# Output projection, two normalisations, turn and router products in one stage over tiles of 128 tokens

## The chip, the cores and the metric

The kernel runs on one core of a Trainium2 chip. The metric is the time of one execution in microseconds (us); the median of three runs of the kernel before is 3086.5 us (3078.68 to 3088.62).

## The reference, cut to what matters

Two transformer blocks follow one another on 512 tokens of width 1024, batch 1, all in float32. Each block is a mixer and then a mixture of experts. The change concerns the end of each mixer and the first step of each mixture of experts.

```python
# block one, after the mixer's two branches (attention and LRU)
mixed = jnp.concatenate([rms_norm(attn, g_attn), rms_norm(lru, g_lru)], axis=-1)
mix = jnp.einsum('bse,ed->bsd', mixed, w_out)                    # 512x1024 @ 1024x1024
x = layer_norm(DEEPNORM_ALPHA * x + (1.0 + gt_m) * mix, ln1_g[l], ln1_b[l])
u = layer_norm(x) * (1.0 + sc_f) + sh_f
#   router of block one: u @ w_grp (4 columns), u @ w_exp (16 columns), then softmax and top k

# block two, after its two attention branches
y = (sigmoid(g_a) * (o_a @ w_out_a) + sigmoid(g_b) * (o_b @ w_out_b)) @ w_o   # the last one: 512x1024 @ 1024x1024
x = x + gt1 * rmsnorm(y, g_post_mix[i])
h2 = rmsnorm(x, g_pre_ffn[i]) * (1 + sc2) + sh2
#   router of block two: h2 @ w_router (32 columns), then top 4 and softmax
```

## The kernel before

The part of the program that the change touches is, in block one, this chain of stages; in block two it is the same with other names:

1. `norm_branches` ("nb1", line 1111) normalises the two branches and turns them into the stationary operand `mixed`; SP loads the first two chunks of `w_out` meanwhile. In block two its place is taken by `turn` ("tz", line 496).
2. `out_projection` ("out1", line 1384), in block two `project` ("out2"): the weight goes by in four chunks of 256 output columns. For each chunk the four token tiles are multiplied (16 outputs of 128 x 256, 24 matmuls each), so that a tile of tokens is complete only when the last chunk has gone by. In block one VectorE takes each output from PSUM with lines 1391 and 1392, in block two ScalarE copies it (line 2807).
3. `normalise` ("n1b" / "n2y", line 413): statistics of all four tiles, then the scaling of all four, on VectorE.
4. `normalise` ("m1n" / "m2n"), called from `moe_inputs`: the same again with the modulation's rows; each tile is stored to `xn_dram`.
5. `turn` ("m1t" / "m2t"): 32 transposes of 128 x 128 on TensorE, copied out of PSUM by ScalarE (line 531).
6. `route` ("r1" / "r2", line 1414): SP loads the router's weights, TensorE makes 32 products of 128 x 20 (block two 128 x 32) at line 1468, VectorE adds the bias at line 1511 and a long chain of small operations follows, which ends in the list of experts for the next stage.

## Time and profile before

| | |
|---|---|
| median of three runs | 3086.5 us (3078.68 to 3088.62) |
| the profiled execution's own time | 3086.95 us |
| its span in the profile | 3085.2 us |
| PE, PEld, DVE, ACT, POOL busy | 82%, 67%, 73%, 51%, 11% of the span |
| mean granted TensorE clock | 0.908 |
| HBM traffic | 692.73 MB read, 39.39 MB written |

Engines: PE is TensorE's matmuls, PEld its weight loads, DVE is VectorE, ACT is ScalarE, POOL is GpSimd, SP issues most DMAs. The clock is a share of 2.4 GHz and has two levels, 1.00 and 0.50 (1.2 GHz). The page's 40 slices are 77 us each; the two stretches in question lie in slices 6 and 7 and in slices 21 and 22, where DMA is at 1 or 2 tenths; the slices with DMA at 9 tenths are the two expert loops. The chain that ended last on the page covers only the program's last few operations, so the stretches are read from the timeline and the windows.

### The profile page before, as it was taken

The page shows a single profiled execution, that of the slowest core. Times are in us where ns is not written, and L with a number is a line of the kernel's source. Part 1 is how long each engine was busy: PE and PEld are TensorE (multiplying, and loading weights), DVE is VectorE, ACT ScalarE, POOL GpSimd, SP SyncE. Part 2 cuts the span into 40 slices and gives each one's busy share as a digit, 9 for nine tenths or more (in the row PEclk, how much of TensorE's full clock was granted, in tenths as well). Part 3 has the DMA queues.
Part 4 walks back from the last instruction along what each step waited for, and adds up shares of the span by engine and source line. Part 5 has one row for each costly group of instructions (what it writes and reads, how often), then busy time and mean ns, then how long its engine had stood idle before and what let it go on. Part 6 is the DMA issues. An engine that isn't in the chain of part 4 may idle for free. (4 is left out here: it accounts for less than half of the span.)

```text
span 3085.2 us, 37604 instructions
## 1 busy us (share of the span) xinstructions
PE 2534.3 (82%) x12807; PEld 2078.8 (67%) x12807; DVE 2238.1 (73%) x2195; ACT 1573.6 (51%) x1462; POOL 339.5 (11%) x277
## 2 busy tenths in 40 slices
PE   2968773599991999778873599999999999999991
PEld 2852663477771999567673477777777777777771
DVE  5637754588885440678535699999999999999985
ACT  2213620477763531546230366776777777776770
POOL 1110200033330000000000001111011111112110
PEclk9989885799995999889985699999999999999995
DMA  5846111699993341000221699999999999999984
GB/s 194 271 137 222 23 61 56 244 362 377 370 361 131 94 134 49 1 28 1 82 69 43 217 352 367 369 368 365 363 368 366 364 366 360 366 365 366 367 332 156
DMA packets 254856, 731.70 MB, mean 237 GB/s; under 512 B 29772, under 2 KB 69931, under 8 KB 252527
## 3 DMA queue, kind: packets, MB, share of 16 engines
q1 hardware_dynamic: 228180, 645.62, 57.9%
q0 software_dynamic: 21984, 80.77, 6.9%
q10 hardware_dynamic: 4608, 4.20, 0.4%
q8 instruction: 51, 0.84, 0.1%
q14 instruction: 33, 0.27, 0.0%
HBM read 692.73 MB, written 39.39 MB: 237 GB/s over the span
## 5 line engine op out<-in xcount | busy, mean ns | idle before, releaser
L48 PE MATMUL psum_all<-sb_ring_r,sb_arena_r 128*128 128x512 f32 (+1 forms) x2912 | 1070.9, 368 | 0.0
L154 DVE TENSOR_TENSOR sb_ring_r<-sb_ring,sb_hi_ring 128x2048 fp32r<-128x2048 f32 x297 | 674.7, 2288 | 207.4 <-ACT sb_hi_ring L145 201.8
L47 PE MATMUL psum_all<-sb_hi_ring,sb_arena_r 128*128 128x512 f32 (+1 forms) x1880 | 666.9, 355 | 53.7 <-DVE sb_ring_r L154 46.6
L49 PE MATMUL psum_all<-sb_hi_ring,sb_arena_r 128*128 128x512 f32 (+1 forms) x1880 | 661.0, 352 | 0.0
L48 PEld LDWEIGHTS psum_all<-sb_ring_r,sb_arena_r 128*128 128x128 f32 x2912 | 558.5, 192 | 91.0
L145 ACT ACTIVATE sb_hi_ring<-sb_ring 128x2048 fp32r<-128x2048 f32 x297 | 564.4, 1914 | 108.0 <-DMA sb_ring<-in_w_gu_dram 34.1
L154 DVE TENSOR_TENSOR sb_ring_r<-sb_ring,sb_arena_r 128x2048 fp32r<-128x2048 f32 x258 | 582.0, 2285 | 31.5 <-ACT sb_arena_r L145 30.9
L145 ACT ACTIVATE sb_arena_r<-sb_ring 128x2048 fp32r<-128x2048 f32 x258 | 485.4, 1911 | 199.9 <-DMA sb_ring<-in_w_gu_dram 192.5
L47 PEld LDWEIGHTS psum_all<-sb_hi_ring,sb_arena_r 128*128 128x128 f32 x1880 | 362.3, 193 | 110.3 <-DVE sb_ring_r L154 51.9
L47 PE MATMUL psum_all<-sb_arena_r 128*128 128x512 f32 x1032 | 417.3, 404 | 11.8 <-DVE sb_ring_r L154 6.8
L49 PE MATMUL psum_all<-sb_arena_r 128*128 128x512 f32 x1032 | 408.2, 396 | 0.0
L49 PEld LDWEIGHTS psum_all<-sb_hi_ring,sb_arena_r 128*128 128x128 f32 x1880 | 361.2, 192 | 51.1
L47 PEld LDWEIGHTS psum_all<-sb_arena_r 128*128 128x128 f32 x1032 | 194.9, 189 | 68.7 <-DVE sb_ring_r L154 27.5
L49 PEld LDWEIGHTS psum_all<-sb_arena_r 128*128 128x128 f32 x1032 | 195.8, 190 | 45.7
L1723 POOL DMA_INDIRECT y_dram<-sb_arena x52 | 89.3, 1718 | 989.9 <-ACT sb_arena L1874 989.9
L1709 POOL COPY sb_arena<-sb_ids 128x1 int32 (+1 forms) x54 | 28.7, 531 | 1034.2 <-POOLq L70 467.5
L47 PE MATMUL psum_all<-sb_arena_r,sb_hi_ring 128*128 128x512 f32 (+2 forms) x232 | 90.1, 389 | 38.5 <-DVE sb_hi_ring L781 30.6
L1849 ACT ACTIVATE sb_arena_r<-psum_all 128x1024 fp32r<-128x1024 f32 x54 | 55.2, 1022 | 114.6 <-PE psum_all L1752 96.2
L1924 DVE TENSOR_TENSOR sb_arena_r<-psum_all,sb_arena_r 128x1024 fp32r<-128x1024 f32 x54 | 65.6, 1214 | 62.8 <-ACT sb_arena_r L1849 62.8
L512 PE MATMUL psum_all<-sb_ident,sb_arena 128*128 128x128 f32 x128 | 29.1, 394 | 91.1 <-PEq L70 89.3
L1869 ACT ACTIVATE sb_arena_r<-psum_all 128x1024 fp32r<-128x1024 f32 (+1 forms) x52 | 45.8, 881 | 106.7 <-PE psum_all L1761 106.5
L1714 POOL DMA_INDIRECT sb_arena<-xn_dram,sb_arena x54 | 92.9, 1720 | 65.4 <-POOL sb_arena L1709 40.8
(393 smaller groups left out, 3159.1 us busy)
## 6 DMA issues: line engine op xcount, KB each, us to landing
sb_ring<-in_w_gu_dram SPq DMA_DIRECT2D x272, 1024.0 KB, 6.9
sb_ring<-in_w_dn_dram SPq DMA_DIRECT2D x136, 1024.0 KB, 9.5
sb_ring<-in_w_e_gate_dram SPq DMA_DIRECT2D x36, 1024.0 KB, 7.3
sb_ring<-in_w_e_up_dram SPq DMA_DIRECT2D x36, 1024.0 KB
sb_ring<-in_w_e_down_dram SPq DMA_DIRECT2D x36, 1024.0 KB, 7.4
sb_ring<-in_w_in_dram SPq DMA_DIRECT2D x27, 1024.0 KB, 7.0
sb_arena<-in_w_ada_dram POOLq DMA_DIRECT2D x16, 1024.0 KB, 5.8
sb_ring<-in_w_mod_dram SPq DMA_DIRECT2D x16, 1024.0 KB, 5.2
```

The source lines that it names most:

```text
L47: eng.matmul(out, a[0], b[0], start=start, stop=False)
L48: eng.matmul(out, a[0], b[1], start=False, stop=False)
L49: return eng.matmul(out, a[1], b[0], start=False, stop=stop)
L145: act.activation(s.hi[c % len(s.hi)], s.raw[c % len(s.raw)], ACT.Copy).then_inc(s.hi_made, 1)
L154: dve.tensor_tensor(s.lo[c % len(s.lo)], s.raw[c % len(s.raw)], s.hi[c % len(s.hi)].bitcast(F32), ALU.subtract).then_inc(s.lo_made, 1)
L512: ins = pe.transpose(k.psum[:, i % 2, t * P:(t + 1) * P], src[:, t, i * P:(i + 1) * P], k.ident[:])
L1709: pool.tensor_copy(idx, R.ids[:, bass.ds(j, 1)]).then_inc(s.idx, 1)
L1714: pool.indirect_dma_start(xg, None, m.x, bass.IndirectOffsetOnAxis(ap=idx.bitcast(U32), axis=0)).then_inc(s.gathered, 16)
L1723: pool.indirect_dma_start(m.y, bass.IndirectOffsetOnAxis(ap=to_row.bitcast(U32), axis=0), ysb.rearrange("p h n -> p (h n)"), None).then_in ...
L1849: act.activation(part, banks, ACT.Copy).then_inc(s.x_hi, 1)
L1869: act.activation(part, banks, ACT.Copy).then_inc(s.h_hi, 1)
L1924: dve.tensor_tensor(part, banks, turned_banks(x_hi[p], KD)[0].bitcast(F32), ALU.subtract).then_inc(s.x_lo, 1)
```

## The change

The stages 2 to 5 of the list above and the router's products of stage 6 become one stage, `project_and_normalise`, called once per block. The weight is loaded in four chunks of 256 rows (all 1024 columns) instead of four chunks of 256 columns, all four of them in the stage before (`ahead`), and its high and low halves all stay in SBUF. TensorE then multiplies one tile of 128 tokens with the whole weight (48 matmuls of 128 x 512 into two PSUM banks), and VectorE and ScalarE normalise that tile twice while TensorE works on the next. Each finished tile is transposed by TensorE (8 transposes), copied by ScalarE and multiplied with the router's weights (8 products). The rows of gain and shift and the router's weights are loaded at the start of this stage. In block two the sums of squares come from ScalarE (`Square` with an accumulator) and no longer from VectorE's batch statistics. `route` begins with the addition of the bias.

The diff, cut to its core ("first" is true in block one):

```diff
-                  ahead=[column_chunk(a["w_out"][0], 256 * h) for h in range(AHEAD)],
+                  ahead=[row_chunk(a["w_out"][0], c) for c in range(4)],
-    out_projection(nc, k, "out1", a["w_out"][0], mixed, k.gate_rows[0:1, :], k.arena[:, 0:D])
-    normalise(nc, k, "n1b", k.x, TT, D, k.x, True, 1e-5, gain=a["ln1_g"][0], bias=a["ln1_b"][0])
-def out_projection(nc, k, name, w, mixed, gate_dram, gate):
...
+    rows = [k.rows[:, 0, :]] + [k.arena[:, 20480 + D * i:20480 + D * (i + 1)] for i in range(4)]
+    project_and_normalise(nc, k, "out1", True, mixed, k.arena_r[:, 8192:10240], area(10240, 2, D),
+                          list(zip(rows, (k.gate_rows[0], a["ln1_g"][0], a["ln1_b"][0], k.gate_rows[5], k.gate_rows[4]))),
+                          [(a["w_grp"][0], a["b_grp"][0]), (a["w_exp"][0], a["b_exp"][0])], area(0, TT, D), area(4096, KD, T))
...
+def row_chunk(w, c):
+    return w[256 * c:256 * c + 256, :].rearrange("(k p) n -> p k n", p=P)
...
+def project_and_normalise(nc, k, name, first, mixed, fourth, tmp, rows, routers, xn, u):
...
+    hi = [k.hi_ring[:, i, :] for i in range(HI_SLOTS)] + [fourth]
+    raw, lo = [k.ring[:, i, :] for i in range(4)], [k.ring_lo[:, i, :] for i in range(4)]
+    two = lambda t: x_rows(k.psum[:, 2 * (t % 2):2 * (t % 2) + 2, :])
+    x_rows = lambda ap: ap.rearrange("p a n -> p (a n)")
...
+        @block.sync
+        def _(sp):
+            for dst, src in rows:
+                sp.dma_start(dst, src.partition_broadcast(P)).then_inc(s.rows, 16)
+            c = 0
+            for ws, bs in routers:
+                n = ws.shape[1]
+                sp.dma_start(router[:, :, c:c + n], ws.rearrange("(k p) n -> p k n", p=P),
+                             allow_slow_non_contiguous=True).then_inc(s.router, 16)
+                sp.dma_start(bias[:, c:c + n], bs.partition_broadcast(P)).then_inc(s.router, 16)
+                c += n
+            for t in range(TT):
+                sp.wait_ge(s.done, t + 1)
+                sp.dma_start(k.xn_dram[t * P:(t + 1) * P, :], xn[:, t, :]).then_inc(s.stored, 16)
+            sp.wait_ge(s.stored, 16 * TT)
+            sp.wait_ge(s.router, 32 * len(routers))
+        @block.tensor
+        def _(pe):
+            def multiply(t):
+                if t >= 2:
+                    pe.wait_ge(s.emptied, t - 1)
+                for kk in range(KD):
+                    c, j = kk // 2, kk % 2
+                    if t == 0 and j == 0:
+                        pe.wait_ge(s.w_lo, c + 1)
+                    a = [x[:, kk, t * P:(t + 1) * P] for x in mixed]
+                    for half in range(2):
+                        b = [x[c][:, j * D + 512 * half:j * D + 512 * half + 512] for x in (hi, lo)]
+                        ins = split3(pe, k.psum[:, 2 * (t % 2) + half, :], a, b, kk == 0, kk == KD - 1)
+                ins.then_inc(s.multiplied, 1)
+            def turn_tile(t):
+                pe.wait_ge(s.done, t + 1)
+                if t >= 1:
+                    pe.wait_ge(s.put, t)
+                for kk in range(KD):
+                    ins = pe.transpose(k.psum[:, 4 + kk // 4, (kk % 4) * P:(kk % 4) * P + P], xn[:, t, kk * P:(kk + 1) * P],
+                                       k.ident[:])
+                ins.then_inc(s.turned, 1)
+            def score(t):
+                if t == 0:
+                    pe.wait_ge(s.router, 32 * len(routers))
+                pe.wait_ge(s.put, t + 1)
+                for kk in range(KD):
+                    ins = pe.matmul(k.psum[:, 7, t * W:(t + 1) * W], u[:, kk, t * P:(t + 1) * P], router[:, kk, :],
+                                    start=kk == 0, stop=kk == KD - 1)
+            multiply(0)
+            multiply(1)
+            multiply(2)
+            turn_tile(0)
+            multiply(3)
+            score(0)
+            for t in range(1, TT):
+                turn_tile(t)
+                score(t)
+        @block.scalar
+        def _(act):
+            def square(t, src, out, total, done):
+                act.activation(out, src, ACT.Square, accum_out=total[:, t:t + 1]).then_inc(done, 1)
+            def root(t, inv, out, ready, done):
+                act.wait_ge(ready, t + 1)
+                act.activation(out[:, t:t + 1], inv[:, t:t + 1], ACT.Sqrt).then_inc(done, 1)
+            def put(t):
+                act.wait_ge(s.turned, t + 1)
+                act.activation(u[:, :, t * P:(t + 1) * P], x_rows(k.psum[:, 4:6, :]).rearrange("p (k n) -> p k n", k=KD),
+                               ACT.Copy).then_inc(s.put, 1)
+            def mixed_in(t):
+                if not first:
+                    act.wait_ge(s.multiplied, t + 1)
+                    square(t, two(t), tmp[:, t % 2, :], squares1, s.squared1)
+                root(t, inv1, root1, s.inverted1, s.rooted1)
+            def taken_out(t):
+                if not first:
+                    act.wait_ge(s.mixed, t + 1)
+                    square(t, k.x[:, t, :], xn[:, t, :], squares2, s.squared2)
+                root(t, inv2, root2, s.inverted2, s.rooted2)
+            for c in range(4):
+                act.activation(hi[c], raw[c], ACT.Copy).then_inc(s.w_hi, 1)
+            mixed_in(0)
+            taken_out(0)
+            mixed_in(1)
+            taken_out(1)
+            mixed_in(2)
+            put(0)
+            taken_out(2)
+            mixed_in(3)
+            put(1)
+            taken_out(3)
+            put(2)
+            put(3)
+        @block.vector
+        def _(dve):
+            link = chain(dve, s.chain)
+            def invert(t, src, scale, eps, inv, ready):
+                link(dve.tensor_scalar(inv[:, t:t + 1], src, scale, eps, ALU.mult, ALU.add))
+                dve.reciprocal(inv[:, t:t + 1], inv[:, t:t + 1]).then_inc(ready, 1)
+            def centred(t, inv, ready):
+                x = k.x[:, t, :]
+                dve.bn_stats(stats[:, t, 0, :], x[:, 0:512])
+                link(dve.bn_stats(stats[:, t, 1, :], x[:, 512:D]))
+                link(dve.bn_aggr(aggr[:, t, :], stats[:, t, :, :]))
+                invert(t, aggr[:, t, 1:2], 1.0, 1e-5, inv, ready)
+            def mix_in(t):
+                x, part = k.x[:, t, :], tmp[:, t % 2, :]
+                if first:
+                    gate = rows[0][0]
+                    dve.wait_ge(s.multiplied, t + 1)
+                    dve.tensor_tensor(part, two(t), gate, ALU.mult).then_inc(s.emptied, 1)
+                    dve.wait_ge(s.emptied, t + 1)
+                    link(dve.scalar_tensor_tensor(out=x, in0=x, scalar=ALPHA, in1=part, op0=ALU.mult, op1=ALU.add))
+                    centred(t, inv1, s.inverted1)
+                    return
+                dve.wait_ge(s.squared1, t + 1)
+                invert(t, squares1[:, t:t + 1], 1.0 / D, 1e-6, inv1, s.inverted1)
+            def normalise(t):
+                x, part = k.x[:, t, :], tmp[:, t % 2, :]
+                if first:
+                    gain, shift = rows[1][0], rows[2][0]
+                    link(dve.scalar_tensor_tensor(out=x, in0=x, scalar=aggr[:, t, 0:1], in1=gain, op0=ALU.subtract,
+                                                  op1=ALU.mult))
+                    dve.wait_ge(s.rooted1, t + 1)
+                    link(dve.scalar_tensor_tensor(out=x, in0=x, scalar=root1[:, t:t + 1], in1=shift, op0=ALU.mult,
+                                                  op1=ALU.add))
+                    centred(t, inv2, s.inverted2)
+                    return
+                gain = rows[0][0]
+                dve.wait_ge(s.rooted1, t + 1)
+                dve.scalar_tensor_tensor(out=part, in0=two(t), scalar=root1[:, t:t + 1], in1=gain, op0=ALU.mult,
+                                         op1=ALU.mult).then_inc(s.emptied, 1)
+                dve.wait_ge(s.emptied, t + 1)
+                dve.tensor_tensor(x, x, part, ALU.add).then_inc(s.mixed, 1)
+            def mean_out(t):
+                if not first:
+                    dve.wait_ge(s.squared2, t + 1)
+                    invert(t, squares2[:, t:t + 1], 1.0 / D, 1e-6, inv2, s.inverted2)
+            def take_out(t):
+                x, out, scale, shift = k.x[:, t, :], xn[:, t, :], rows[3 - (not first)][0], rows[4 - (not first)][0]
+                dve.wait_ge(s.rooted2, t + 1)
+                if first:
+                    link(dve.scalar_tensor_tensor(out=out, in0=x, scalar=aggr[:, t, 0:1], in1=scale, op0=ALU.subtract,
+                                                  op1=ALU.mult))
+                    dve.scalar_tensor_tensor(out=out, in0=out, scalar=root2[:, t:t + 1], in1=shift, op0=ALU.mult,
+                                             op1=ALU.add).then_inc(s.done, 1)
+                    return
+                link(dve.scalar_tensor_tensor(out=out, in0=x, scalar=root2[:, t:t + 1], in1=scale, op0=ALU.mult,
+                                              op1=ALU.mult))
+                dve.tensor_tensor(out, out, shift, ALU.add).then_inc(s.done, 1)
+            for c in range(4):
+                dve.wait_ge(s.w_hi, c + 1)
+                dve.tensor_tensor(lo[c], raw[c], hi[c].bitcast(F32), ALU.subtract).then_inc(s.w_lo, 1)
+            dve.wait_ge(s.rows, 16 * len(rows))
+            if not first:
+                link(dve.tensor_tensor(rows[0][0], rows[0][0], rows[1][0], ALU.mult))
+            for t in range(TT):
+                mix_in(t)
+                if t >= 1:
+                    take_out(t - 1)
+                normalise(t)
+                mean_out(t)
+            take_out(TT - 1)
...
         def _(pe):
-            pe.wait_ge(s.loaded, 32 * len(routers))
-            for t in range(TT):
-                for kk in range(KD):
-                    ins = pe.matmul(k.psum[:, 0, t * W:(t + 1) * W], u[:, kk, t * P:(t + 1) * P], w[:, kk, :],
-                                    start=kk == 0, stop=kk == KD - 1)
-            ins.then_inc(s.scored, 1)
...
-            dve.wait_ge(s.scored, 1)
-            psum = k.psum[:, 0, 0:TT * W].rearrange("p (t w) -> p t w", t=TT)
+            psum = k.psum[:, 7, 0:TT * W].rearrange("p (t w) -> p t w", t=TT)
...
-def moe_inputs(nc, k, name, centre, eps, scale, shift):
...
-    normalise(nc, k, name + "n", k.x, TT, D, xn, centre, eps, gain=scale, bias=shift,
-              store=[k.xn_dram[t * P:(t + 1) * P, :] for t in range(TT)])
-    turn(nc, k, name + "t", xn, TT, KD, None, None, None, None, plain=u)
-    return u
...
 def block_one_moe(nc, k, a):
-    u = moe_inputs(nc, k, "m1", True, 1e-5, k.gate_rows[5], k.gate_rows[4])
     k.route.max_items = 23
-    route(nc, k, "r1", u, [(a["w_grp"][0], a["b_grp"][0]), (a["w_exp"][0], a["b_exp"][0])], 16, 2, 4)
+    route(nc, k, "r1", 16, 2, 4)
...
-    y = area(12288, TT, D)
-    turn(nc, k, "tz", z, TT, KD, None, None, *zt, order=from_grid,
-         ahead=[column_chunk(a["w_o_2"][0], 256 * h) for h in range(AHEAD)])
-    project(nc, k, "out2", [dict(src=column_chunk(a["w_o_2"][0], 256 * h), uses=[use_t(y, 0, 256 * h, zt, T)])
-                            for h in range(D // 256)], ahead=AHEAD)
-    normalise(nc, k, "n2y", y, TT, D, k.x, False, 1e-6, gain=a["g_post_mix_2"][0], gate=k.gate_rows[2])
+    turn(nc, k, "tz", z, TT, KD, None, None, *zt, order=from_grid, ahead=[row_chunk(a["w_o_2"][0], c) for c in range(4)])
+    rows = [k.arena[:, 20480 + D * i:20480 + D * (i + 1)] for i in range(4)]
+    project_and_normalise(nc, k, "out2", False, zt, k.arena_r[:, 16384:18432], area(18432, 2, D),
+                          list(zip(rows, (a["g_post_mix_2"][0], k.gate_rows[2], k.gate_rows[7], k.gate_rows[6]))),
+                          [(a["w_router_2"][0], a["b_router_2"][0])], area(0, TT, D), area(12288, KD, T))
```

How TensorE's list stands at the end of the stretch in block one, before: the projection, then in the stages after it ("L67" and the line behind it are the barrier) the 32 transposes of stage 5 and the 32 router products of stage 6.

```order
L48 MATMUL psum_all<-sb_ring_r,sb_arena_r 128x256
L49 MATMUL psum_all<-sb_hi_ring,sb_arena_r 128x256
L67 UNCONDITIONAL_BRANCH
L506 UNCONDITIONAL_BRANCH
L512 MATMUL psum_all<-sb_ident,sb_arena 128x128 x32
L67 UNCONDITIONAL_BRANCH
L1463 UNCONDITIONAL_BRANCH
L1468 MATMUL psum_all<-sb_arena 128x20 x32
```

The same place after the change, from the last matmul of the fourth token tile on (L1467 is the transpose of a tile, L1476 its router products):

```order
L49 MATMUL psum_all<-sb_arena_r 128x512
L1476 MATMUL psum_all<-sb_rows,sb_arena 128x20 x8
L1467 MATMUL psum_all<-sb_ident,sb_arena 128x128 x8
L1476 MATMUL psum_all<-sb_rows,sb_arena 128x20 x8
L1467 MATMUL psum_all<-sb_ident,sb_arena 128x128 x8
L1476 MATMUL psum_all<-sb_rows,sb_arena 128x20 x8
L1467 MATMUL psum_all<-sb_ident,sb_arena 128x128 x8
L1476 MATMUL psum_all<-sb_rows,sb_arena 128x20 x8
L67 UNCONDITIONAL_BRANCH
```

Three of the four transposes and all router products stand behind the last projection matmul; only the first tile's transpose has moved up, in front of the fourth tile's matmuls.

VectorE's list in block one, before, from the end of the projection to the route: each kind of operation for all tiles, in a stage of its own.

```order
L1392 SCALAR_TENSOR_TENSOR sb_x<-sb_x,sb_pair 128x256
L67 UNCONDITIONAL_BRANCH
L442 UNCONDITIONAL_BRANCH
L447 BN_STATS sb_small<-sb_x 128x6 x8
L450 BN_AGGR sb_small<-sb_small 128x2 x4
L453 TENSOR_SCALAR sb_small<-sb_small 128x4
L458 RECIPROCAL sb_small<-sb_small 128x4
L466 SCALAR_TENSOR_TENSOR sb_x<-sb_x,sb_small,sb_rows 128x1024 x4
L472 SCALAR_TENSOR_TENSOR sb_x<-sb_x,sb_small,sb_rows 128x1024 x4
```

After, the operations for the second tile (L1550 and L1552 take it from PSUM, L1585 and L1587 finish the tile before it, L1562 and L1565 scale it):

```order
L1550 TENSOR_TENSOR sb_arena<-psum_all,sb_rows 128x1024
L1552 SCALAR_TENSOR_TENSOR sb_x<-sb_x,sb_arena 128x1024
L1540 BN_STATS sb_small<-sb_x 128x6
L1541 BN_STATS sb_small<-sb_x 128x6
L1542 BN_AGGR sb_small<-sb_small 128x2
L1535 TENSOR_SCALAR sb_small<-sb_small 128x1
L1536 RECIPROCAL sb_small<-sb_small 128x1
L1585 SCALAR_TENSOR_TENSOR sb_arena<-sb_x,sb_small,sb_arena 128x1024
L1587 SCALAR_TENSOR_TENSOR sb_arena<-sb_arena,sb_small 128x1024
L1562 SCALAR_TENSOR_TENSOR sb_x<-sb_x,sb_small,sb_arena 128x1024
L1565 SCALAR_TENSOR_TENSOR sb_x<-sb_x,sb_small,sb_arena 128x1024
```

The work of four stages now stands tile by tile in one list, and a tile's last two operations come behind the first ones of the next tile.

## Rows read from the trace of the kernel before

**Rows 1.** Timeline: start, us, engine, line, operation; where the two stretches begin and end.
```profile
412.21 3.71 ACT L145 ACTIVATE sb_hi_ring<-sb_ring 128x2048 fp32r<-128x2048 f32 x2 [2.97 <-PEq L70]
526.53 0.24 DVE L1511 TENSOR_TENSOR sb_arena<-psum_all,sb_arena 128x80 f32<-128x80 f32 x1 [30.11 <-PE psum_all L1468]
...
1560.02 3.71 ACT L145 ACTIVATE sb_hi_ring<-sb_ring 128x2048 fp32r<-128x2048 f32 x2 [1.44 <-PEq L70]
1676.28 0.29 DVE L1511 TENSOR_TENSOR sb_arena<-psum_all,sb_arena 128x128 f32<-128x128 f32 x1 [29.30 <-PE psum_all L1468]
```

**Rows 2.** Windows, block one: length, PE, PEld, DVE, ACT, POOL busy; clock, DMA.
```profile
411.90:464.30 52.40, 46.45 (x384) 46.25 (x384) 22.38 (x36) 7.55 (x4) 0.00 (x0) 0.93 0.17 51
464.30:480.60 16.30, 0.00 (x0) 0.00 (x0) 15.24 (x22) 0.21 (x1) 0.00 (x0) 0.59 0.18 64
480.60:500.60 20.00, 0.04 (x1) 0.07 (x2) 15.24 (x22) 0.21 (x1) 0.00 (x0) 0.50 0.43 158
500.60:508.00 7.40, 6.21 (x32) 4.91 (x32) 0.00 (x0) 4.60 (x8) 0.00 (x0) 0.71 0.01 2
508.00:526.50 18.50, 13.84 (x64) 13.73 (x64) 0.00 (x0) 1.28 (x1) 0.00 (x0) 0.60 0.07 5
```

**Rows 3.** Timeline of PE: start of both projections, and 512-column matmuls in the expert loop.
```profile
416.50 0.58 PE L47 MATMUL psum_all<-sb_hi_ring,sb_arena_r 128*128 128x256 f32 x1 [22.06 <-DVE sb_ring_r L154]
419.63 0.28 PE L49 MATMUL psum_all<-sb_hi_ring,sb_arena_r 128*128 128x256 f32 x1
...
1564.31 0.58 PE L47 MATMUL psum_all<-sb_hi_ring,sb_arena_r 128*128 128x256 f32 x1 [7.52 <-DVE sb_ring_r L154]
1569.96 0.28 PE L49 MATMUL psum_all<-sb_hi_ring,sb_arena_r 128*128 128x256 f32 x1
...
579.88 0.39 PE L48 MATMUL psum_all<-sb_ring_r,sb_arena_r 128*128 128x512 f32 x1
580.11 0.39 PE L49 MATMUL psum_all<-sb_hi_ring,sb_arena_r 128*128 128x512 f32 x1
```

**Rows 4.** Timeline of DVE in the stage that combines block one's experts, tile by tile.
```profile
960.14 1.23 DVE L2160 TENSOR_TENSOR sb_arena<-sb_arena,sb_rows 128x1024 f32<-128x1024 f32 x1
...
962.66 0.69 DVE L2162 BATCH_NORM_STATS2 sb_small<-sb_x 128x6 f32<-128x512 f32 x1
...
964.50 1.28 DVE L2156 SCALAR_TENSOR_TENSOR sb_arena<-sb_arena,sb_weight 128x1024 f32<-128x1024 f32 x1
...
970.18 1.26 DVE L2172 SCALAR_TENSOR_TENSOR sb_x<-sb_x,sb_small,sb_rows 128x1024 f32<-128x1024 f32 x1
...
972.68 1.28 DVE L2156 SCALAR_TENSOR_TENSOR sb_arena<-sb_arena,sb_weight 128x1024 f32<-128x1024 f32 x1
```

**Rows 5.** Timeline of ACT in the same stage: a square with its accumulator.
```profile
989.40 1.06 ACT L2126 ACTIVATE sb_arena<-sb_x 128x1024 f32<-128x1024 f32 x1 [2.30 <-DVE sb_x L2174]
990.36 0.19 ACT L2126 ACTIVATION_READ_ACCUMULATOR sb_arena<-sb_x 128x1 f32 x1
```

**Rows 6.** The page's groups that read two PSUM banks in the expert loops.
```profile
L1849 ACT ACTIVATE sb_arena_r<-psum_all 128x1024 fp32r<-128x1024 f32 x54 | 55.2, 1022 | 114.6 <-PE psum_all L1752 96.2
L1924 DVE TENSOR_TENSOR sb_arena_r<-psum_all,sb_arena_r 128x1024 fp32r<-128x1024 f32 x54 | 65.6, 1214 | 62.8 <-ACT sb_arena_r L1849 62.8
```

**Rows 7.** Timeline of PE: the last 8 transposes of block one's turn.
```profile
505.83 1.16 PE L512 MATMUL psum_all<-sb_ident,sb_arena 128*128 128x128 f32 x8 [0.18 <-ACT sb_arena L531]
```

**Rows 8.** Timeline of DVE: the first operation after a barrier.
```profile
464.66 4.84 DVE L447 BATCH_NORM_STATS2 sb_small<-sb_x 128x6 f32<-128x512 f32 x8 [0.79 <-PEq L70]
```

**Rows 9.** Windows (last two columns: DMA share, GB/s): row broadcasts; chunks of w_o.
```profile
482.00:486.00 4.00, 0.00 (x0) 0.00 (x0) 3.97 (x8) 0.00 (x0) 0.00 (x0) 0.50 0.80 256
...
1552.00:1554.00 2.00, 1.87 (x8) 1.35 (x8) 1.03 (x2) 1.94 (x5) 0.00 (x0) 0.50 1.03 327
```

**Rows 10.** Timeline of SP: the loads ahead, in block one and in block two.
```profile
383.88 1.04 SPq L1124 DMA_DIRECT2D sb_ring<-in_w_out_dram  x2
...
1548.49 1.75 SPq L123 DMA_DIRECT2D sb_ring<-in_w_o_dram  x2
```

47 lines of the change are left out of this document (19 added, 28 removed).

## The prediction

> **What bounds the kernel now.** I read the page first. The chain of waits there covers only the program's tail, so it says nothing about the middle. I went to the timeline of each engine around the two projections, then to the windows. A stage starts only after a barrier, so inside each stretch every microsecond between its first and last instruction is on the path. Each stretch begins where ScalarE rounds the first chunk of the projection's weight and ends where VectorE adds the router's bias, behind which the unchanged route runs: 526.53 - 412.21 = 114.3 us in block one and 1676.28 - 1560.02 = 116.3 us in block two [rows 1]. The windows of block one [rows 2] show the engines taking turns: 52.4 us in which TensorE is busy for 46.45 and VectorE for 22.38; two stretches of 16.3 and 20.0 us with VectorE alone (15.24 in each; the second also waits for stores); 7.4 us of transposes; 18.5 us of router products, 13.84 of them busy and the rest a wait for the router's weights. In a stretch of 114.3 us TensorE has 66.5 us of work and VectorE 52.9 (the columns added up), so about half can go if the two overlap. Everything outside the stretches keeps its instructions.
>
> **What the profile bases the sum on.** The profiled execution took 3086.95 us by itself, its span and the little that lies around it, and the median of the runs is 3086.5: I subtract from 3086.95 and expect no offset between that and a median.
>
> **The parts, block one.** All times below are on the clock of the trace before.
>
> Start. The first chunk has 128x2048 values as before, so TensorE's first matmul stays at 416.50 [rows 3]. Two further chunks are now loaded by the stage before. That stage begins its loads at 383.88 [rows 10] and ends at the barrier before 412.21; 4.2 MB at the 327 GB/s of rows 9 are 12.8 us plus about 1.5 until data flow, so they are in by 399: no cost. If that cover were gone, they would cost up to 12 us.
>
> Matmuls. 384 of 256 columns become 192 of 512. The start-to-start time of 512 columns at the full clock is 580.11 - 579.88 = 0.233 us [rows 3], together 44.8 us. Before, TensorE began cold and ran at the high level from 419.63, 3.1 us later [rows 3]; half of that is lost, 1.6 us. VectorE delivers a low half in about 2.4 us (twice the 1.21 of rows 6, the width being double) against 2.8 us or more of matmuls per chunk, so tile 0 doesn't wait. Tile 0 is complete at 429.2; tile 3 at 416.5 + 44.8 + 1.6 + 1.2 (the first tile's 8 transposes in between [rows 7]) = 464.1. So the product costs what it cost.
>
> VectorE per tile. Taking the tile from PSUM, adding, statistics and inverse: from 960.14 to 964.50 the same seven operations take 4.36 [rows 4], with the multiply reading PSUM, which costs 1.21 while TensorE streams [rows 6]. Scaling: two operations, 972.68 - 970.18 = 2.5 [rows 4], then statistics 964.50 - 962.66 = 1.84 [rows 4]: 4.35 with the link. Finishing: 2.5. Together 11.2 us, the same as TensorE's 48 x 0.233 = 11.2 per tile: the two are even, and VectorE has slack only through the transposes. At the end it owes for tile 3: 4.36, then tile 2's finish 2.5, 4.35, 2.5, so it is done at 464.3 + 13.7 = 478.0.
>
> Tail of TensorE. Its list is in order: router products of tile 0, then transpose, copy, products for tiles 1, 2, 3. A tile's products are 16 of the 64 instructions in 13.84 us [rows 2], 3.5 us, at the low level. A transpose of a tile is 1.16 at the high level [rows 7]; the other 24 of the 32 took 5.05, and I take 2.0 at the low level, an estimate from these. The copy is 1.02 [rows 6] plus 0.2 of handover. ScalarE's copy of tile 1 stands behind its root for tile 3, which waits for VectorE's first 4.36 us: 469.0. From there: copy 470.1, products 473.5, transpose 475.4, copy 476.9, products 480.4, transpose 482.4 (VectorE's tile 3 was ready at 478.0, so it is not waited for), copy 483.5, products 487.1. A barrier and the first instruction behind it cost 0.8 to 0.9 [rows 8]: the bias is added at 488.0 instead of 526.5. Gain 38.5 us.
>
> Loads in the stage. Five rows of 512 KB at 256 GB/s [rows 9] are 10.2 us, so 424.2 with the start, before tile 0 is complete at 429.2; the router's weights follow and are wanted after 464: no cost. Each is now issued ahead of its need, where it was waited for in stage 6 (18.50 - 13.84 = 4.7 us of rows 2, part of the gain). The four stores ride beside the next tile; the last one is issued at 478.0 and is over before 487. If the rows landed at 158 GB/s, the mean of the window with stores [rows 2], they would be in at 431, a 2 us delay of VectorE that the tail of TensorE hides.
>
> **The parts, block two.** Here the stage before is short and the loads are not hidden. The issue begins at 1548.49 [rows 10]; 4.2 MB at 327 GB/s end at about 1562.3, and that stage used to end some 0.8 before 1560.02, at 1559.2. The stretch starts 3.0 us later, at 1563.0 (bounds 0 and 13 more, the latter at half that rate). Then: first matmul 4.3 later [rows 3], 44.8 + 1.2, and 5.65 us of cold start [rows 3], half lost, 2.8: tile 3 complete at 1616.1. VectorE has four wide operations per tile instead of six plus statistics, ScalarE two squares of 1.06 + 0.19 [rows 5]; a tile takes them about 8 us against TensorE's 11.2, so both wait for TensorE. After tile 3: square 1.4, inverse 0.4, tile 2's finish 2.5, scaling 2.5, square 1.5, inverse and root 0.8, finish 2.5: done at 1627.9. TensorE's own list takes longer: products of tile 0 to 1617.9, transpose 1619.1, copy 1620.2, products 1623.8, transpose and copy 1627.0, products 1630.5, transpose and copy 1633.7, products 1637.2, barrier: 1638.1 instead of 1676.3. Gain 38.2 us.
>
> Sum: 3086.95 - 38.5 - 38.2 = 3010.
>
> **A rule on the clock, weighed.** The window 500.60:508.00 holds transposes as TensorE's only work, and its mean clock is 0.71; it starts at 0.50, so the clock rose while transposing. The next window is router products alone, busy for 13.84 us, and has a mean of 0.60, so the clock fell before them and stayed at 1.2 GHz although the engine was never idle [rows 2]. The Trainium skill ("TensorE: Matmul & The Clock Gate", Part 4: PE-mode transpose) says that the full clock doesn't engage for transposes. This trace, whose transposes are of float32, doesn't agree. By the rule the tail is at 1.2 GHz throughout, which is my sum; the rows leave it open.
>
> **Rivals.**
> (1) The tail runs at 2.4 GHz. For: the tail starts warm, and transposes alternate with products [rows 2]. Against: products alone ran at the low level. Price: three products at 1.75 less and three transposes at 0.85 less, then the end is set by VectorE: in block one 478.0 + 1.2 + 1.1 + 1.75 + 0.4 + 0.9 = 483.4, in block two 1627.9 + 5.3 = 1633.2. Time 3001.
> (2) Transfers hold the stages back: four chunks through the short stage of block two at half the rate (9 us more), and in block one rows that land late, 2 to 4 us. For: DMA was idle there before, so no row shows 6 MB in a queue. Against: 327 GB/s with two chunks in flight. Time about 3023.
> (3) TensorE stays at 1.2 GHz during the matmuls as well. For: it now waits for VectorE more often, since a tile costs both 11.2 us. Price: 512 columns at 1.2 GHz are 0.427 us, so 192 of them 82 us, 35 more than in my sum: block one ends at 524 and block two at 1674, 2 us gained in each: 3083, no change. Against: in the projection before, the clock was at 0.93 with the same waits of VectorE on the other side. It decides only if VectorE were late by some microseconds in every tile. The Trainium skill ("TensorE: Matmul & The Clock Gate", HAM oscillation) warns of just this: gaps between groups of matmuls send the clock down again and again. No gap longer than the transposes is in my schedule, so by this rule too the matmuls stay warm.
> (4) Slower than before: VectorE's and ScalarE's wide operations slow down by a factor f while TensorE fills the other two PSUM banks. Block one then ends at 439 + 45 f, block two at about 1591 + 34 f. At f = 2.5 that is 551 and 1676: 25 us lost in block one, nothing gained in block two, time 3111. It turns to a loss from f = 2.2. Against: VectorE's 1.21 and ScalarE's 1.02 from two PSUM banks were measured beside a busy TensorE [rows 6], f = 1.
>
> **How the numbers follow.** Forecast 3010, chance 0.63, own range 3003 to 3017 (cold start 3 to 6 us, load 0 to 4 more, handovers). Rival 1: 0.16; rival 2: 0.17; rival 3: 0.02; rival 4: 0.02. The range 2998 to 3029 takes in the first three. Faster by over 0.3% (9 us, about what this kernel's measurement tells from no change): 0.96. Same: 0.02. Slower: 0.02.
>
> **What would show it.** In the changed kernel's timeline: the first 512-column matmul 4.3 us after the stage's first rounding; tiles 11.2 us apart; VectorE idle for under 2 us per tile in block one and for 3 or more in block two; the clock of the window behind the last matmul (0.5: forecast; 1.0: rival 1); bias additions 76 and 75 us after the stages' start; the stage before block two's longer by 3 us. It would be wrong if the fourth tile's matmuls waited for VectorE, or if an expert loop changed its length.

## The result

| | before | changed kernel |
|---|---|---|
| median | 3087.49 us (3078.68 to 3088.62, 4 runs) | 3000.43 us (2997.26 to 3005.29, 4 runs) |
| ratio, 95% interval | | 0.9723, 0.971 to 0.9737 |
| profiled execution, its span | 3086.95, 3085.2 us | 2997.26, 2995.5 us |
| mean granted clock | 0.908 | 0.921 |
| PE, PEld, DVE, ACT, POOL busy | 82%, 67%, 73%, 51%, 11% | 84%, 68%, 74%, 53%, 11% |
| HBM read, written | 692.73, 39.39 MB | 692.73, 39.39 MB |

The forecast was 3010 us, between 2998 and 3029. The median lies 9.6 us under the point, inside that range, and 2.6 us under the narrower range of 3003 to 3017 that I gave for the stage's own terms. The mechanism was the one forecast. The median alone couldn't have said so: it is the time that rival 1 gave (3001), and the traces show that rival 1's tail didn't come. The two medians differ by 87 us, more than the change is worth: what follows puts it at 80 to 82 us.

The two stretches of the program, from ScalarE's first rounding of the projection's weight to VectorE's addition of the router's bias, in the timeline of the changed kernel (start, us, engine, line, operation; in brackets the idle time before it and what ended it). They answer to [rows 1]:

```profile
409.35 5.51 ACT L1516 ACTIVATE sb_hi_ring<-sb_ring 128x2048 fp32r<-128x2048 f32 x3 [2.98 <-PEq L70]
484.60 0.24 DVE L1688 TENSOR_TENSOR sb_arena<-psum_all,sb_rows 128x80 f32<-128x80 f32 x1 [9.41 <-PEq L70]
1512.77 3.71 ACT L1516 ACTIVATE sb_hi_ring<-sb_ring 128x2048 fp32r<-128x2048 f32 x2 [3.56 <-PEq L70]
1585.61 0.29 DVE L1688 TENSOR_TENSOR sb_arena<-psum_all,sb_rows 128x128 f32<-128x128 f32 x1 [9.31 <-PEq L70]
```

Block one's stretch is 484.60 - 409.35 = 75.25 us where it was 114.32; block two's is 72.84 where it was 116.26. The bracket on line 1688 shows where the new stage is bound at its end: VectorE has been done for 9.4 us and waits at the barrier for TensorE (PEq).

The windows answer to [rows 2]: length, then busy time of PE, PEld, DVE, ACT and POOL, the granted clock, DMA. The first and the third run to the last of the wide products (the projection's 128x512 matmuls), the second and the fourth from there to the bias:

```profile
409.35:460.75 51.40, 47.11 (x202) 38.04 (x202) 39.40 (x50) 9.44 (x11) 0.00 (x0) 0.93 0.21 74
460.75:484.60 23.85, 17.10 (x89) 15.94 (x87) 13.59 (x18) 3.29 (x6) 0.00 (x0) 0.58 0.11 45
1512.77:1565.30 52.53, 48.24 (x200) 38.86 (x201) 24.10 (x27) 17.52 (x24) 0.00 (x0) 0.91 0.19 63
1565.30:1585.60 20.30, 15.98 (x89) 14.79 (x87) 7.98 (x10) 5.66 (x10) 0.00 (x0) 0.63 0.13 52
```

Before, VectorE was busy for 22.38 us beside block one's products and for the rest of its 52.9 us alone. Now it is busy for 39.40 us beside them and 13.59 us are left behind. The products themselves cost what they did: 51.4 us from the start of the stretch here, 52.1 there (464.30 - 412.21). A clock of 0.58 and 0.63 in the two tails says that TensorE ran mostly at 1.2 GHz in them.

VectorE takes the tiles from PSUM at these times in block one:

```profile
426.61 1.22 DVE L1550 TENSOR_TENSOR sb_arena<-psum_all,sb_rows 128x1024 f32<-128x1024 f32 x1 [6.42 <-PE psum_all L49]
437.71 1.23 DVE L1550 TENSOR_TENSOR sb_arena<-psum_all,sb_rows 128x1024 f32<-128x1024 f32 x1 [2.21 <-PE psum_all L49]
449.04 1.21 DVE L1550 TENSOR_TENSOR sb_arena<-psum_all,sb_rows 128x1024 f32<-128x1024 f32 x1
460.91 1.23 DVE L1550 TENSOR_TENSOR sb_arena<-psum_all,sb_rows 128x1024 f32<-128x1024 f32 x1 [0.48 <-PE psum_all L49]
```

The tiles are 11.1 to 11.9 us apart, and the waits of VectorE are 2.21, none and 0.48 us: it and TensorE are even, as the prediction had it. A tile costs VectorE a little more than the 11.2 us of the forecast: between the second and the third row it didn't wait, and they lie 11.33 us apart. The operation that reads two PSUM banks takes 1.21 to 1.23 us, so nothing slowed down beside TensorE (rival 4).

TensorE's tail in block one, the router products (L1476; the 8 products of a tile stand in the trace as 16 instructions) and the transposes (L1467):

```profile
460.71 1.86 PE L1476 MATMUL psum_all<-sb_rows,sb_arena 128*128 128x20 f32 x16
462.41 1.07 PE L1467 MATMUL psum_all<-sb_ident,sb_arena 128*128 128x128 f32 x8
466.55 3.60 PE L1476 MATMUL psum_all<-sb_rows,sb_arena 128*128 128x20 f32 x16 [3.06 <-ACT sb_arena L1500]
469.98 1.95 PE L1467 MATMUL psum_all<-sb_ident,sb_arena 128*128 128x128 f32 x8
473.52 3.60 PE L1476 MATMUL psum_all<-sb_rows,sb_arena 128*128 128x20 f32 x16 [1.59 <-ACT sb_arena L1500]
476.95 1.95 PE L1467 MATMUL psum_all<-sb_ident,sb_arena 128*128 128x128 f32 x8
480.01 3.60 PE L1476 MATMUL psum_all<-sb_rows,sb_arena 128*128 128x20 f32 x16 [1.11 <-ACT sb_arena L1500]
```

The first two groups ran at 2.4 GHz, the others at 1.2: the same 16 products take 1.86 us and then 3.60, the same 8 transposes 1.07 and then 1.95. In front of each products group TensorE waits for ScalarE's copy (L1500), 3.06 us the first time. In that wait the copy stood in ScalarE's queue behind a root, as these two rows of ScalarE show; the transposes that it copies had ended at 463.5:

```profile
465.38 0.20 ACT L1496 ACTIVATE sb_small<-sb_small 128x1 f32<-128x1 f32 x1 [4.71 <-DVE sb_small L1536]
465.49 1.01 ACT L1500 ACTIVATE sb_arena<-psum_all 128x1024 f32<-128x1024 f32 x1
```

In block two the clock held a little longer, so that the second products group took 2.43 us and not 3.62, and that tail is 20.3 us long where block one's is 23.9:

```profile
1565.32 1.87 PE L1476 MATMUL psum_all<-sb_rows,sb_arena 128*128 128x32 f32 x16
1567.02 1.07 PE L1467 MATMUL psum_all<-sb_ident,sb_arena 128*128 128x128 f32 x8
1569.20 2.43 PE L1476 MATMUL psum_all<-sb_rows,sb_arena 128*128 128x32 f32 x16 [1.11 <-ACT sb_arena L1500]
1571.45 1.95 PE L1467 MATMUL psum_all<-sb_ident,sb_arena 128*128 128x128 f32 x8
```

The stage before block two's now loads four pieces. Its first load is issued 14.00 us before the stretch starts (1498.77 to 1512.77); before it was 11.53 [rows 1, 10]: 2.5 us given back. Over both blocks the change is worth 39.07 + 43.42 - 2.47 = 80.0 us in the trace. The spans differ by 89.7. The other 9.7 us lie in four places whose instructions are the same, but for two more loads ahead of block one's stretch: 2.9 there (412.21 to 409.35), 5.3 in the expert loop behind it, 2.5 between that loop and block two's first load, and -1.0 behind block two's stretch. They have to be explained or to be shown as variation.

### The profile page after: what moved, and what is told of

It reads as the page before. It is cut to its first block and busy times, and to the rows that moved or that the text cites. A ratio compares the mean times of both kernels' runs of the same rounds, so it can differ in the third digit from the quotient of the medians.

```text
span 2995.5 us, 36673 instructions
## 1 busy us (share of the span) xinstructions
PE 2524.9 (84%) x12423; PEld 2051.6 (68%) x12423; DVE 2229.2 (74%) x2169; ACT 1573.9 (53%) x1466; POOL 329.5 (11%) x277
## 3 DMA queue, kind: packets, MB, share of 16 engines
HBM read 692.73 MB, written 39.39 MB: 244 GB/s over the span
## 5 line engine op out<-in xcount | busy, mean ns | idle before, releaser
L48 PE MATMUL psum_all<-sb_ring_r,sb_arena_r 128*128 128x512 f32 (+1 forms) x2784 | 1048.9, 377 | 0.0
L154 DVE TENSOR_TENSOR sb_ring_r<-sb_ring,sb_hi_ring 128x2048 fp32r<-128x2048 f32 x289 | 656.3, 2287 | 184.9 <-ACT sb_hi_ring L145 179.1
L47 PE MATMUL psum_all<-sb_hi_ring,sb_arena_r 128*128 128x512 f32 (+1 forms) x1720 | 632.3, 368 | 57.3 <-DVE sb_ring_r L1596 32.1
L49 PE MATMUL psum_all<-sb_hi_ring,sb_arena_r 128*128 128x512 f32 (+1 forms) x1720 | 627.0, 365 | 0.0
L48 PEld LDWEIGHTS psum_all<-sb_ring_r,sb_arena_r 128*128 128x128 f32 x2784 | 532.9, 191 | 96.4
L145 ACT ACTIVATE sb_hi_ring<-sb_ring 128x2048 fp32r<-128x2048 f32 x289 | 547.9, 1912 | 85.4 <-DMA sb_ring<-in_w_gu_dram 30.5
L47 PE MATMUL psum_all<-sb_arena_r 128*128 128x512 f32 x1064 | 429.8, 404 | 12.2 <-DVE sb_ring_r L154 7.5
L49 PE MATMUL psum_all<-sb_arena_r 128*128 128x512 f32 x1064 | 420.3, 395 | 0.0
L47 PEld LDWEIGHTS psum_all<-sb_hi_ring,sb_arena_r 128*128 128x128 f32 x1720 | 330.3, 192 | 119.0 <-DVE sb_ring_r L1596 32.5
L49 PEld LDWEIGHTS psum_all<-sb_hi_ring,sb_arena_r 128*128 128x128 f32 x1720 | 329.2, 191 | 56.1
L47 PEld LDWEIGHTS psum_all<-sb_arena_r 128*128 128x128 f32 x1064 | 200.9, 189 | 70.7 <-DVE sb_ring_r L154 27.9
L49 PEld LDWEIGHTS psum_all<-sb_arena_r 128*128 128x128 f32 x1064 | 201.9, 190 | 47.0
L1886 POOL COPY sb_arena<-sb_ids 128x1 int32 (+1 forms) x54 | 22.4, 415 | 945.4 <-POOLq L70 428.0
L1018 ACT ACTIVATE sb_hi_ring<-psum_all 128x512 fp32r<-128x512 f32 (+3 forms) x144 | 64.7, 478 | 60.6 <-PE psum_all L958 59.0
```

What stands on the lines that cost most here:

```text
L47: eng.matmul(out, a[0], b[0], start=start, stop=False)
L48: eng.matmul(out, a[0], b[1], start=False, stop=False)
L49: return eng.matmul(out, a[1], b[0], start=False, stop=stop)
L145: act.activation(s.hi[c % len(s.hi)], s.raw[c % len(s.raw)], ACT.Copy).then_inc(s.hi_made, 1)
L154: dve.tensor_tensor(s.lo[c % len(s.lo)], s.raw[c % len(s.raw)], s.hi[c % len(s.hi)].bitcast(F32), ALU.subtract).then_inc(s.lo_made, 1)
L1018: act.activation(dst, src, ACT.Copy).then_inc(s.rounded, 1)
```

## The experiments

Times of the traces below are cut at the same marks in every kernel. "Loop 1" is from the first bias addition to SP's first load of `y_dram`, and holds block one's route and expert loop; the tail is the part of a stretch behind its last wide product; "short" is from block two's first load ahead to the start of its stretch. Medians are of 4 to 10 runs, the ratios are to the runs of the kernel before on the same chip. Medians of different rows can come from different chips, on which the kernel before had 3083.75 to 3087.49 us; there the ratios are the safer comparison. (The texts of the expectations count the loop from a later mark: their 396 and 391 us are the 425.2 and 419.9 of this table.)

| kernel | median, us | ratio (95%) | stretch 1 (tail) | loop 1 | short | stretch 2 (tail) |
|---|---|---|---|---|---|---|
| before | 3087.49 | 1 | 114.32 | 425.20 | 11.53 | 116.26 |
| changed | 3000.43 | 0.9723 (0.971 to 0.9737) | 75.25 (23.9) | 419.88 | 14.00 | 72.84 (20.3) |
| changed, again | 3003.28 | 0.9729 (0.9708 to 0.9749) | 75.25 (23.9) | 428.75 | 13.92 | 72.93 (20.4) |
| block one alone | 3045.49 | 0.9866 (0.9845 to 0.9886) | 75.13 (23.9) | 429.98 | 11.53 | 116.49 |
| block two alone | 3043.92 | 0.9867 (0.9848 to 0.9886) | 114.57 | 422.08 | 14.19 | 72.97 (20.3) |
| no overlap | 3080.29 | 0.9978 (0.9964 to 0.9992) | 117.45 | 432.42 | 13.98 | 106.22 |
| no overlap, clock kept up | 3067.61 | 0.9947 (0.9928 to 0.9966) | 110.38 | 428.49 | 13.85 | 99.71 |
| clock kept up in the tail | 2997.22 | 0.9724 (0.9706 to 0.9741) | 71.13 (19.8) | 422.83 | 13.71 | 67.53 (16.1) |
| two pieces ahead | 3003.13 | 0.9726 (0.9707 to 0.9745) | 75.41 (23.9) | 429.42 | 11.91 | 72.76 (20.9) |
| new order in the tail | 3003.88 | 0.9738 (0.9713 to 0.9762) | 73.45 (22.0) | 425.09 | 13.89 | 72.61 (21.3) |
| the three together | 2991.10 | 0.9694 (0.9677 to 0.9712) | 71.22 (19.9) | 423.05 | 11.44 | 67.33 (14.7) |
| and a warm start | 2987.43 | 0.9689 (0.9667 to 0.9712) | 69.43 (19.5) | 426.02 | 11.44 | 65.03 (14.7) |

### Where the gain stands, and the 9.7 us outside the stretches

*Block one alone* keeps block two's old stages:

```
- turn(nc, k, "tz", ..., ahead=[row_chunk(a["w_o_2"][0], c) for c in range(4)])
- project_and_normalise(nc, k, "out2", False, ...)
+ turn(nc, k, "tz", ..., ahead=[column_chunk(a["w_o_2"][0], 256 * h) for h in range(AHEAD)])
+ project(nc, k, "out2", ...)
+ normalise(nc, k, "n2y", ...)
```

with the old `moe_inputs` and the old `route` for block two. It was expected:

> Block one's stage is the new one, block two keeps its old stages. Theory (each block's gain stands in its own stretch, from the first rounding of the output projection's weight to the first bias addition of the routing, and nowhere else): block one's stretch 75.3 us as in the changed kernel, block two's 116.3 us as before, the whole about 39 us under the kernel before, near 3048. Rival A (the 6 to 9 us by which the medians differ beyond the two stretches come with the changed block one, in the first expert loop and ahead of the stretch): 45 to 48 us under, near 3040, with the first expert loop near 391 us instead of 396. Rival B (the two blocks' gains aren't independent): neither.

*Block two alone* is the same the other way round. It was expected:

> Block two's stage is the new one, block one keeps its old stages. Theory: block one's stretch 114.3 us, block two's 73 us and 1.5 us lost ahead of it to four loads instead of two; the whole about 42 us under the kernel before, near 3045. If the first expert loop takes 396 us here and 391 in the kernel with block one alone, what the changed kernel gained outside the stretches comes with block one's change; if it differs without that pattern, it is variation between executions.

*Changed, again* is the changed kernel itself. It was expected:

> The changed kernel itself once more, for its trace. Theory (what differs outside the two stretches is variation between executions): 3000 us, stretches 75.3 and 72.8 us within 0.5, and a first expert loop that may be 391 or 396 us, a start of the first stretch between 409 and 412. Rival (it belongs to the change): loop 391 us and start 409.4 again, within 1 us.

Each stretch shortens where its stage is new and nowhere else: 75.13 beside 116.49, 114.57 beside 72.97. In the medians, against 3085.13 us for before on the same chip, the two halves gain 39.6 and 41.2 us, together 80.8; the whole gains 81.9 in its second measurement. Sum of the traces' parts: 80.0.

Loop 1 has the same instructions in all of these kernels. It lasts 419.9 to 432.4 us, with no pattern: 430.0 with block one alone, where rival A wanted it short, and 419.9 and 428.8 in two executions of one and the same kernel. The mark at its end in those two, SP's timeline of the changed kernel:

```profile
904.48 0.82 SPq L2278 DMA_DIRECT2D sb_arena<-y_dram  x2
```

and the bias additions at 484.60 and 485.37 before it: 8.9 us of difference for equal code. In the second trace of the changed kernel the stretches and the short stage give 80.0 us as in the first, and its span is 80.9 us under the one before: outside them 0.9 us are left where it was 9.7. So the 9.7 us are variation between executions, of which the first measurement of the changed kernel had the lucky side.

### What the gain is made of

*No overlap* keeps the resident weight, the 512-column products, the single stage and the router products inside, and takes only the concurrency away:

```
                 if t >= 2:
                     pe.wait_ge(s.emptied, t - 1)
+                if t >= 1:
+                    pe.wait_ge(s.done, t)
 ...
                 mix_in(t)
-                if t >= 1:
-                    take_out(t - 1)
                 normalise(t)
                 mean_out(t)
-            take_out(TT - 1)
+                take_out(t)
```

> The changed kernel with the overlap taken out: TensorE starts a tile's products only when VectorE is done with the tile before, and VectorE finishes a tile before it takes the next. Weight in SBUF, 512-wide products, one stage and the router products inside all stay. Theory (the gain is VectorE's and ScalarE's work beside the products): per block three times VectorE's 11.2 us per tile come back, 31 us in block one and 28 in block two, and up to 8 us more in each because TensorE starts each tile's products at 1.2 GHz after its wait; 60 to 75 us over the changed kernel, 3060 to 3075, which is nearly all of the gain of 87. Rival (the gain is the resident weight, the wide products and the fewer barriers, and the overlap is a detail): at most 20 us over the changed kernel.

It gave back 42.2 and 33.4 us in the stretches, and 77 us in the median against the changed kernel's second measurement; of the gain of 2.7%, 0.2% is left. The rival's 20 us are out of question, and the theory's 60 to 75 were passed by a little. PE's timeline in it, at the first product of the second, third and fourth tile:

```profile
437.28 0.80 PE L47 MATMUL psum_all<-sb_hi_ring,sb_arena_r 128*128 128x512 f32 x1 [11.93 <-DVE sb_arena L1589]
463.22 0.76 PE L47 MATMUL psum_all<-sb_hi_ring,sb_arena_r 128*128 128x512 f32 x1 [11.95 <-DVE sb_arena L1589]
488.23 0.77 PE L47 MATMUL psum_all<-sb_hi_ring,sb_arena_r 128*128 128x512 f32 x1 [11.08 <-DVE sb_arena L1589]
```

TensorE waits for VectorE for 11.1 to 11.95 us, where the forecast had 11.2 us per tile. The windows of one wait and of the products behind it:

```profile
425.30:437.20 11.90, 0.04 (x1) 0.00 (x0) 11.09 (x16) 0.41 (x2) 0.00 (x0) 0.67 0.00 0
437.20:451.30 14.10, 13.99 (x48) 10.84 (x48) 0.02 (x1) 0.00 (x0) 0.00 (x0) 0.80 0.09 37
```

The 48 products need 14.0 us here and 11.2 without a wait before them, because the clock (0.80 in the mean) starts at 1.2 GHz.

*No overlap, clock kept up* splits the two. In the waits TensorE makes products that nobody reads, into PSUM bank 6, which the stage doesn't use:

```
                 if t >= 1:
+                    for _ in range(44 if first else 33):
+                        pe.matmul(k.psum[:, 6, :], mixed[0][:, 0, 0:P], hi[0][:, 0:512], start=True, stop=True)
                     pe.wait_ge(s.done, t)
```

> The kernel without overlap once more, with 128x512 products that nobody reads in TensorE's waits between the tiles (44 in block one, 33 in block two, 0.233 us each), so that its clock stays up. It splits what the missing overlap cost (117.5 us against 75.3 in block one, 106.2 against 72.8 in block two). Theory (of each tile's 14.0 us of products after a wait, 2.8 are the fall to 1.2 GHz and 11.2 the products themselves): three tiles by 2.8 us come back in each block, stretches 109 and 98, 3064; the rest, 34 and 25 us, is VectorE's and ScalarE's work standing beside nothing. Rival (the slow start of a tile has another cause, weights or semaphores): stretches as they were, 117 and 106, 3080.

```profile
440.73 0.50 PE L47 MATMUL psum_all<-sb_hi_ring,sb_arena_r 128*128 128x512 f32 x1 [1.67 <-DVE sb_arena L1591]
452.00 10.43 PE L1454 MATMUL psum_all<-sb_hi_ring,sb_arena_r 128*128 128x512 f32 x44
464.02 0.50 PE L47 MATMUL psum_all<-sb_hi_ring,sb_arena_r 128*128 128x512 f32 x1 [1.59 <-DVE sb_arena L1591]
```

The products of the second tile run from 440.73 to 452.00, 11.3 us. The stretches lose 7.1 and 6.5 us, where 8 were expected in each. With 110.38 and 99.71 us as the stretches of a stage without overlap whose clock doesn't fall between the tiles, the gain divides so: overlap 110.38 - 75.25 = 35.1 us in block one and 99.71 - 72.84 = 26.9 in block two; all the rest together (fewer barriers, the router's weights loaded in time, one stage for the two passes of statistics, in block two no copy of the projection to SBUF by ScalarE and back) 3.9 and 16.6 us. Which of the things in the brackets these are was not tried. That "no overlap" had lost nearly everything is thus two losses: 62 us of overlap, and 14 us of clock, which a kernel without overlap pays at the start of each tile.

Behind these rows stands a rule: the Trainium skill ("TensorE: Matmul & The Clock Gate", HAM oscillation) says that a wait between groups of products lets the clock fall, so that each group starts cold. The trace agrees: the first product behind each of six waits of 8.0 to 11.95 us took 0.76 to 0.80 us, beside 0.50 where the clock was kept up, and of the 13.6 us that came back 12.5 lie ahead of the last wide product (94.2 us against 87.1 in block one, 85.4 against 80.05 in block two), 2.1 for each of the six.

### The tail

*Clock kept up in the tail* puts the same unread products where TensorE waits behind the last tile:

```
             for t in range(1, TT):
                 turn_tile(t)
+                keep_busy(n)     # 12, 16, 4 products in block one; 4, 10, 4 in block two
                 score(t)
```

> The changed kernel with products that nobody reads (128x512, into a free PSUM bank) in TensorE's waits behind the last tile's products: 12 before the second tile's router products, 16 before the third's, 4 before the fourth's in block one, and 4, 10 and 4 in block two. Theory (the narrow router products let the clock fall to 1.2 GHz, and wide work in the waits keeps it at 2.4): every router product group near 1.9 us instead of 3.6, transposes near 1.1 instead of 1.95, the tail bounded by VectorE's last tile: bias additions 4.3 and 4.2 us earlier, 8 to 9 us in all, near 2992. Rival (the clock falls all the same and the fillers take 0.43 us each): the tails 2 to 6 us longer in each block, 3004 to 3012.

```profile
464.32 1.85 PE L1476 MATMUL psum_all<-sb_rows,sb_arena 128*128 128x20 f32 x16
466.02 1.07 PE L1467 MATMUL psum_all<-sb_ident,sb_arena 128*128 128x128 f32 x8
466.84 3.04 PE L1481 MATMUL psum_all<-sb_hi_ring,sb_arena_r 128*128 128x512 f32 x12
470.15 1.96 PE L1476 MATMUL psum_all<-sb_rows,sb_arena 128*128 128x20 f32 x16 [0.28 <-ACT sb_arena L1506]
```

The second products group now takes 1.96 us instead of 3.60, the waits stay as long as they were but are filled, and both tails have a mean clock of 1.00:

```profile
464.32:484.07 19.75, 17.94 (x121) 15.35 (x119) 13.60 (x19) 3.30 (x6) 0.00 (x0) 1.00 0.13 54
1567.00:1582.95 15.95, 14.50 (x106) 12.55 (x105) 7.97 (x10) 5.67 (x10) 0.00 (x0) 1.00 0.17 67
```

The tails are 4.1 and 4.2 us shorter, where 4.3 and 4.2 were expected (the other 1.1 us of block two's stretch lie at its start, below); the median moved by 3.2 to 6 us, according to which measurement of the changed kernel it is set against. The ratio, 0.9724, can't be told from the changed kernel's 0.9723 and 0.9729, so this gain is shown by the traces and not by the times. No run separates what the waits and what the narrow products have to do with the fall of the clock: the unread products changed both.

*New order in the tail* changes only who goes first:

```
             for t in range(TT):                 # VectorE
+                if t == TT - 1:
+                    take_out(t - 1)
                 mix_in(t)
-                if t >= 1:
+                if 1 <= t < TT - 1:
                     take_out(t - 1)
 ...
             taken_out(2)                         # ScalarE, block one
-            mixed_in(3)
-            put(1)
-            taken_out(3)
-            put(2)
+            put(1)
+            mixed_in(3)
+            put(2)
+            taken_out(3)
             put(3)
```

> No fillers; only the order at the end: VectorE finishes the third tile before it takes the fourth's products, and ScalarE copies the second and third tiles' transposes out before it waits for the fourth tile's roots. Theory (in the tail TensorE, at 1.2 GHz, waits for copies that stand in ScalarE's queue behind a root, and VectorE waits 5.2 us in block two while the third tile lies ready): block one's bias addition 2.6 us earlier, block two's 2 to 4 us earlier, 4 to 6 us in all, near 2995. Rival (the tail is bound by VectorE's last tile alone): block one unchanged, block two 2.2 us earlier.

Block one gained 1.8 us of the 2.6 expected, block two 0.2 instead of 2 to 4: for block two a miss, by theory and rival alike. VectorE was in fact done 2 us sooner there (8.9 us after the last wide product, before 11.0), but TensorE's timeline shows that nothing came of it:

```profile
1571.54 1.86 PE L1476 MATMUL psum_all<-sb_rows,sb_arena 128*128 128x32 f32 x16
1573.24 1.07 PE L1467 MATMUL psum_all<-sb_ident,sb_arena 128*128 128x128 f32 x8
1575.43 3.62 PE L1476 MATMUL psum_all<-sb_rows,sb_arena 128*128 128x32 f32 x16 [1.11 <-ACT sb_arena L1500]
1578.86 1.95 PE L1467 MATMUL psum_all<-sb_ident,sb_arena 128*128 128x128 f32 x8
1581.92 3.62 PE L1476 MATMUL psum_all<-sb_rows,sb_arena 128*128 128x32 f32 x16 [1.11 <-ACT sb_arena L1500]
1585.36 1.95 PE L1467 MATMUL psum_all<-sb_ident,sb_arena 128*128 128x128 f32 x8
```

No transposes group waits for VectorE; the chain of transposes, copy and products ran as early as it could at 1.2 GHz, as it did in the changed kernel. The second products group found the clock already down (3.62 us, where it was 2.43), and the tail is 1.0 us longer than the changed kernel's. On the other side the wide products ended 1.2 us sooner, 51.3 us after the stretch's start instead of 52.5. The two go together in block two: 52.5 and 20.3 us, 51.9 and 20.9 (two pieces ahead), 51.3 and 21.3, each adding up to 72.6 to 72.9. Where the clock rose earlier it fell earlier: the first wide products ran at 1.2 GHz for 5.6 us in the changed kernel and for 3.0 in this one, and the fall came inside the second products group there and ahead of it here. So at the low clock block two's tail is bound by TensorE's own chain, not by anyone's order.

*Two pieces ahead*, in block two, loads the third and fourth piece of the weight in the new stage, ahead of its other loads, and ScalarE waits for them before it rounds:

```
- turn(nc, k, "tz", ..., ahead=[row_chunk(a["w_o_2"][0], c) for c in range(4)])
+ turn(nc, k, "tz", ..., ahead=[row_chunk(a["w_o_2"][0], c) for c in range(2)])
 ...
+            for c, src in late:     # SP, first in the stage
+                sp.dma_start(k.ring[:, c, :].rearrange("p (a b) -> p a b", a=2), src).then_inc((s.late2, s.late3)[c - 2], 16)
```

> Block two's weight with two pieces loaded in the short stage before and two in the new stage, instead of all four in the short one. Theory (the short stage waits for its transfers): the short stage back from 13.1 to 11.5 us, the two late pieces land before their rounding is due, 1.5 us gained, 2998.5, hardly to be told from no change in the median and plain in the trace. Rival (the late pieces, 2 MB behind a barrier with four row loads and router loads at their side, land after they are wanted): the stretch up to 3 us longer and the whole 0 to 2 us slower.

The short stage went from 14.0 to 11.9 us and the stretch stayed at 72.76, so the late pieces landed in time: ScalarE waited 1.32 us for the third and 0.65 for the fourth, and TensorE, from its first product on, for none. That is 2.1 us. The median (3003.13, beside 3000.43 and 3003.28) can't show so little; the trace can.

*The three together*, with 4; 4 and 14; and 4 unread products in block one (the 14 ahead of the last transposes), and 4, 4, 4 in block two:

> Order, two pieces ahead in block two, and fillers together (4; 4 and 14; 4 in block one, 4, 4, 4 in block two). Theory: the clock holds, the tail is VectorE's last tile and one tile's transposes, copy and products: bias additions 4.6 and 5.8 us earlier and 1.5 us of loading, 12 us in all, 2988. Rival (clock falls between the fillers): no better than the new order alone, 2993 to 2996.

The short stage is 11.44 us, the tails run at 2.4 GHz nearly throughout, and the median is 2991.10, 9 to 12 us under the changed kernel, where 12 were expected. With the clock up, the new order does bring its share in block two: a tail of 14.7 us, where "clock kept up" alone had 16.1. VectorE was done 8.9 us behind the last wide product instead of 11.0, and the end followed it by 5.8 us instead of 5.2. (The 10 unread products also became 4, but with the 10 the last transposes already started 0.2 us behind VectorE's end, so they held up nothing more.) In block one it brings nothing (19.9 beside 19.8, 0.3 reckoned). In block one 14 unread products took 5.05 us, not 3.3, because the clock fell in them (0.66 in this window), and the last transposes started 0.5 us later behind the last wide product than in the version below with 11:

```profile
476.20:481.20 5.00, 5.00 (x17) 3.97 (x17) 4.04 (x7) 0.20 (x1) 0.00 (x0) 0.66 0.00 0
```

In block two's tail TensorE's list has no wait over 0.2 us left:

```profile
1575.13 1.97 PE L1479 MATMUL psum_all<-sb_rows,sb_arena 128*128 128x32 f32 x16 [0.18 <-ACT sb_arena L1509]
1576.93 1.07 PE L1470 MATMUL psum_all<-sb_ident,sb_arena 128*128 128x128 f32 x8
1577.76 1.18 PE L1484 MATMUL psum_all<-sb_hi_ring,sb_arena_r 128*128 128x512 f32 x4
1579.12 1.97 PE L1479 MATMUL psum_all<-sb_rows,sb_arena 128*128 128x32 f32 x16 [0.18 <-ACT sb_arena L1509]
```

The last version adds *a warm start*, and takes 11 products for the 14:

```
+            for _ in range(9):
+                pe.matmul(k.psum[:, 6, :], mixed[0][:, 0, 0:P], mixed[0][:, 0, :], start=True, stop=True)
             multiply(0)
```

> The combined kernel with nine more unread products (128x512, of the stage's own left factor) at the head of each stage, where TensorE waits 4 us for the weight's first halves, and 11 instead of 14 before block one's last transposes. Theory (the first 13 products of a stage run at 1.2 GHz, 0.43 us each, because TensorE comes from a wait): the slow time is spent in the wait; 1.5 to 2.5 us less in each stretch and 0.5 for the three products, stretches near 69 and 65.5, 3 to 5 us under the combined kernel, 2987. Rival (the start of the products is bound by the halves' arrival, 1.9 us for each piece of the weight, not by the clock): stretches as in the combined kernel, 71.2 and 67.3.

```profile
411.39 4.18 PE L1487 MATMUL psum_all<-sb_arena_r 128*128 128x512 f32 x9 [17.79 <-PEq L70]
415.65 0.50 PE L47 MATMUL psum_all<-sb_hi_ring,sb_arena_r 128*128 128x512 f32 x1
415.99 0.39 PE L48 MATMUL psum_all<-sb_ring_r,sb_arena_r 128*128 128x512 f32 x1
```

The nine fill the 4.3 us wait for the first halves at 1.2 GHz, and the stage's own first product comes at the full clock. The last wide product ends 49.95 and 50.4 us after the start instead of 51.3 and 52.7: 1.4 and 2.3 us, where 1.5 to 2.5 were expected. Block one's tail is 0.4 us shorter for the three products less. The median is 2987.43 us; the runs can't tell it from the three together (0.9689 and 0.9694), but the traces can. It is 13 to 16 us under the changed kernel.

## Why the prediction was right

Counted from the start of each stretch, with the forecast's own steps:

| step | forecast | measured |
|---|---|---|
| block one: last wide product | 51.9 us | 51.4 |
| VectorE done with the fourth tile | 65.8 | 65.8 |
| ScalarE's copy of tile 1, behind the root | 56.8 | 56.1 |
| bias added | 75.8 | 75.25 |
| short stage before block two, longer by | 3.0 | 2.5 |
| block two: last wide product | 53.1 | 52.5 |
| VectorE done with the fourth tile | 64.9 | 63.5 |
| bias added | 75.1 | 72.84 |

**Start and products.** The loads of block one cost nothing. TensorE's first product came 4.3 us after the first rounding in both blocks, and a tile's products took 11.2 us. Both last products were 0.5 to 0.6 us early.

**VectorE per tile.** 11.2 us from the rows of another stage [rows 4] were 11.3 to 11.4 in block one (437.71 to 449.04, and from there to the end of the inverse at 460.43). This is the term on which the forecast rested, and the experiment without overlap showed it naked: waits of 11.1 to 11.95 us. VectorE was idle once for 2.21 us, where the forecast had under 2.

**Tail.** The prediction says that its sum has the tail at 1.2 GHz throughout, from a stretch in which products stood alone [rows 2]. The sum doesn't do it. In block two it takes 1.8 us for tile 0's products and 1.2 for the first transposes (1616.1 to 1617.9 to 1619.1), which are the times at 2.4 GHz; at the 3.5 and 2.0 us of the low level they would have ended at 1621.6, 2.5 us later. In block one they would have ended at 464.1 + 3.5 + 2.0 = 469.6, 0.6 us behind the root that the sum waits for. By its own words the forecast would have been about 3013 us. The trace sides with the sum: these first products and transposes ran at 2.4 GHz, as rival 1 had it, and what came behind the clock's fall at 1.2. In block one the end hangs on the copy behind the root, and that time was right. In block two the whole tail of 20.3 us was forecast as 22.0. This is the term that was mis-sized, by 1.7 us, most of it in tile 1's products: 3.6 us in the sum, and 2.25 in the trace (1569.20 to 1571.45), because the clock fell only inside them.

The row that spoke against rival 1 was read too widely. TensorE came to those products from a wait of 5.65 us, in which the clock was at 1.00 at first (the window) and at 0.50 from about 511.7 on:

```profile
508.00:511.00 3.00, 0.00 (x0) 0.00 (x0) 0.00 (x0) 1.28 (x1) 0.00 (x0) 1.00 0.29 15
512.65 13.63 PE L1468 MATMUL psum_all<-sb_arena 128*128 128x20 f32 x63 [5.65 <-DMA sb_arena<-in_b_exp_dram]
```

So the products stayed at a level that they found, for 13.6 us; the row doesn't say how long they would have kept the high one. What rival 1 would give was measured with the clock kept up: 71.1 us for block one, where it said 483.4 - 412.21 = 71.2, and 67.5 for block two, where it said 1633.2 - 1563.0 = 70.2 (there the last product came 1.7 us sooner than reckoned, and VectorE was done 11.0 us behind it instead of 11.8).

**Loads.** The short stage grew by 2.5 us, forecast 3.0, and rival 2's held rows didn't come: VectorE never waited for them. The experiment with two pieces ahead confirms where the 2.5 us came from.

**Rivals 3 and 4.** The clock was 0.93 and 0.91 over the two groups of wide products, and no operation of VectorE or ScalarE on PSUM lengthened.

**The rest of the distance.** The parts add to 80.0 us, 3.3 more than the 76.7 forecast. From there to the 87 of the first pair of medians it is variation between executions (the second pair of medians gives 81.9), so that two thirds of the 9.6 us between point and median say nothing about the reckoning. The prediction would have called a changed length of an expert loop a sign of being wrong; the loop did move, by 5.3 us, and the second execution of the same kernel moved it back by 8.9. I had expected no offset between the execution profiled and a median, and gave the own range 7 us on either side for the stage's terms alone. A single kernel's runs spread over 5 to 17 us here, and loop 1 over 12.5.

## What to carry to other kernels

When stages stand one behind the other and each keeps one engine busy, add up each engine's busy time over all of them: the largest sum plus the last tile's chain is a first estimate of what a tiled, overlapped stage can reach, and durations from another stage of the same kernel were good to a few tenths for it here. When the clock's level is a term of such a sum, write the level beside each duration: here the words said one level and two of the durations were of the other. A new order for the engine that is last brought nothing while the chain behind it was bound by TensorE's low clock, and 1.5 us once a few unread wide products in TensorE's waits kept the clock up; each of these too many delays what stands behind it. Cut the trace at marks in front of and behind the changed stretch, so that an unchanged part that moved by itself isn't counted as gain.

## What the runs showed of the hardware

- In every tail made of router products, transposes and waits alone the granted clock fell to 1.2 GHz behind the first 16 products and 8 transposes, or inside the next 16, and stayed there, although TensorE was busy for 17.1 of 23.9 us in block one and for 16.0 of 20.3 in block two. With unread products in the waits it stayed at 1.00 in both tails of "clock kept up".
- In block two the clock's rise at the stretch's start and its fall in the tail moved together: 52.5 and 20.3 us, 51.9 and 20.9, 51.3 and 21.3.
- The clock can fall without an idle TensorE: in block one of the kernel with the three together it fell at 477 us, some 11 us behind the last of the stage's wide products, with no wait over 0.42 us in between; it was 0.66 over the window of the 14 wide products and back at 1.00 behind them.
- float32 transposes of 128x128 as TensorE's only work went with a rise of the clock in the kernel before: they started at 500.56 behind 37.6 us of idling, with the clock at 0.50, and from 505 on the clock was at 1.00.
- What the lower clock costs: 16 router products 3.60 us instead of 1.86, 8 transposes 1.95 instead of 1.07, 48 wide products behind a wait 14.0 instead of 11.2.
- An expert loop with indirect transfers took between 419.9 and 432.4 us, its route included, over twelve traced executions of equal instructions.
